# Narrower tiles for the third token tile, and a query projection that does not wait for the norm

## The reference

```python
h = rms(x, norm_mix)                     # x * rstd(x) * norm_mix, rstd is one number per token
proj = h @ w_in                          # split into lru, q_lat, kv_lat, k_rope, ret and mlstm parts
# B: latent attention
q = rms(q_lat, mla_q_norm) @ mla_wq_b    # q_lat is 256 wide
sc = (q_nope . k_nope + q_rope . k_rope) * scale ; p = softmax(sc + chunk mask) ; y_b = p @ v
# C: retention        att = (q k^T) * decay ;  y_c = att @ v + (q S) * cross ; S update
# D: mLSTM            ig, fg = m_if[:, 0:4] + b_i, m_if[:, 4:8] + b_f   (4 heads)
#                     sc = (q k^T) * exp(gates) ; y_d = sc @ v + g * (q C) ; C, n update
x += concat(head_rms(y_a..y_d) * gates) @ w_out
x += SwiGLU(rms(x, norm_ffn)) @ w_down
```

## Time and profile before

| | |
|---|---|
| median of 3 runs | 933.67 us (933.37 to 934.33) |
| the profiled execution | 933.06 us |
| its span, first to last instruction | 931.3 us |
| TensorE busy | 922.5 us, 99% |
| weight loads (PEld) | 811.5 us, 87% |
| VectorE, ScalarE, GpSimd busy | 495.3, 204.2, 444.4 us |
| granted TensorE clock, mean | 0.999 |

### The profile page before, as it was taken

One profiled execution on the slowest core, in us unless ns is written; L12 is line 12 of the kernel. 1 busy time (PEld: TensorE's weight loads), 2 busy tenths in 40 slices (PEclk: granted clock), 3 DMA queues, 4 the chain that ended last, 5 costly groups with the idle time before them and its releaser, 6 DMA issues.

```text
span 931.3 us, 14894 instructions
## 1 busy us (share of the span) xinstructions
PE 922.5 (99%) x5718; PEld 811.5 (87%) x5718; DVE 495.3 (53%) x1009; ACT 204.2 (22%) x445; POOL 444.4 (48%) x469
## 2 busy tenths in 40 slices
PE   8999999999999999999999999999999999999998
PEld 6777877777999999999977678777799999999998
DVE  5474656854565656512253565578357565563221
ACT  2224264531100000100031243562310000110001
POOL 6210380124966666676411205503168666666670
PEclk9999999999999999999999999999999999999999
DMA  9959412119544544443443773112555555534321
GB/s 279 231 132 69 141 47 91 50 15 253 137 136 137 137 137 139 133 146 125 123 128 108 61 147 95 46 48 50 124 149 140 142 144 144 148 123 135 126 95 41
DMA packets 159635, 113.02 MB, mean 121 GB/s; under 512 B 10246, under 2 KB 157356, under 8 KB 159436
## 3 DMA queue, kind: packets, MB, share of 16 engines
q1 hardware_dynamic: 154660, 104.50, 38.8%
q0 software_dynamic: 4272, 6.80, 7.1%
q10 hardware_dynamic: 632, 0.75, 0.3%
HBM read 108.46 MB, written 2.27 MB: 119 GB/s over the span
## 4 chain that ended last, share of the span: by engine, by line
PE 97%; DVE 1%; DMA 1%; ACT 0%; issue 0%; SPq 0%; ACTq 0%; DVEq 0%
PE ps L1128 52%; PE ps L776 20%; PE ps L1085 7%; PE ps L1146 2%; PE ps L885 1%; PE ps L857 1%; PE ps L982 1%; PE ps L922 1%; PE ps L1023 1%; PE ps L1032 1%; PE ps L804 1%; PE ps L824 1%; PE ps L965 1%; DMA arena<-in_x_sample 1%; PE ps L1043 1%; PE ps L1064 0%
## 5 line engine op out<-in xcount | busy, mean ns | idle before, releaser
L776 PE MATMUL ps<-hT,ring 128*128 128x320 f32 x672 | 187.8, 435 | 2.2 <-DVE hT L1597 1.7
L776 PEld LDWEIGHTS ps<-hT,ring 128*128 128x128 f32 x672 | 124.5, 190 | 54.8 <-DVE hT L1597 3.9
L601 POOL TENSOR_TENSOR work<-ring 128x512 f32<-128x512 f32 (+1 forms) x66 | 81.8, 1239 | 154.5 <-issue 113.3
L1128 PE MATMUL ps<-mixT,ring 128*128 128x160 f32 x672 | 105.0, 299 | 0.0
L1128 PE MATMUL ps<-hT,work 128*128 128x160 f32 x672 | 98.5, 299 | 0.0
L1128 PE MATMUL ps<-hT,ring 128*128 128x160 f32 x672 | 98.1, 299 | 0.0
L1128 PEld LDWEIGHTS ps<-mixT,ring 128*128 128x128 f32 x672 | 95.8, 190 | 0.0
L1128 PEld LDWEIGHTS ps<-hT,ring 128*128 128x128 f32 x672 | 93.7, 190 | 0.3
L1128 PEld LDWEIGHTS ps<-hT,work 128*128 128x128 f32 x672 | 93.7, 190 | 0.0
L603 POOL TENSOR_TENSOR work<-ring 128x512 f32<-128x512 f32 (+1 forms) x66 | 82.2, 1246 | 5.2
L602 POOL TENSOR_TENSOR ring<-ring 128x512 f32<-128x512 f32 (+1 forms) x66 | 82.2, 1246 | 5.2
(11 more groups left out here) (392 smaller groups left out, 1351.6 us busy)
## 6 DMA issues: line engine op xcount, KB each, us to landing
ring<-in_w_gu SPq DMA_DIRECT2D x88, 512.0 KB, 5.2
ring<-in_w_in SPq DMA_DIRECT2D x44, 512.0 KB, 7.1
ring<-in_w_down SPq DMA_DIRECT2D x32, 512.0 KB, 4.5
ring<-in_w_out SPq DMA_DIRECT2D x16, 512.0 KB, 4.5
ring<-in_w_down SPq DMA_DIRECT2D x16, 384.0 KB, 3.5
cst<-in_consts POOLq DMA_DIRECT2D x1, 1664.0 KB, 12.3
ring<-in_w_in SPq DMA_DIRECT2D x2, 640.0 KB, 5.5
arena<-r POOLq DMA_DIRECT2D x8, 160.0 KB, 17.0
```

Source lines behind the costliest of these rows:

```text
L601: step(tt(s3, a11, a21, ALU.subtract))
L776: ins = mm(bank(use, 0, T, m), w[:, k, c:c + m], hT[:, k, 0:T], start=(k == 0), stop=(k == KT - 1))
L1128: ins = mm(bank(use, at * HT, HT), left, right(k), start=(opens and k == 0 and at == 0), stop=(closes and k == n - 1), skip_group_check=True)
```

## The change

Four edits, in both layers.

1. Third token tile 64 wide. The third product of `causal_scores` takes 64 key columns as weights in place of 128; VectorE's part of it works on 64 partitions. L817 and L818 of `head_out` take 64 columns of weights and give 64 rows.
2. The turned probabilities. The five pieces that belong to the 64 stream tokens are turned from 64 partitions, 64 columns moving, and packed 64 wide; ScalarE copies 64 and 256 columns in place of 128 and 512.
3. The query latents are projected from `xgm = x * norm_mix` (in the memory of `mixT`), without `rstd`. VectorE multiplies by `rstd` afterwards, in two operations for each half (`qlat_raw`, then `qlT`), and ScalarE squares the first one's result. `xgm` is made by VectorE in layer 0 (8 operations ahead of `normalise`), by ScalarE in layer 1 (one after each square). In layer 1 half of `ql0` is moved ahead of the norm sum. The turn of the gain rows is moved in between the matmuls of `ms1`, and in layer 0 two of the `latents_out` stand ahead of the wait for `cols`. `kvr` now waits for all 8 pieces of `hT`.
4. The input and the forget gate are turned together: three transposes with the forget gate at partition 32 (`mgt`) in place of twice three (`mig`, `mfg`). `mift` is 64 wide and cleared at the start. With one use fewer in the list the later uses swap banks 0 and 1.

```diff
-SCORE_PARTS = ((0, 384), (448, 64))
+SCORE_PARTS = ((0, 384, P), (448, 64, DEC))
-    d("ql0", "ql1", "kvr", "mo0", "mo1", "mig", "mfg", "mv0", "mv1")
+    d("ql0", "ql1", "kvr", "mo0", "mo1", "mgt", "mv0", "mv1")
+        xgm = mixT
-        mift = sb("mift", [P, NT, 2 * H])
+        mift = sb("mift", [P, NT, 64])
@@ TensorE, the sum of ms1
+                if n == 4:
+                    pe.wait_ge(sem("gain_rows"), 16)
+                    nc.tensor.transpose(ps[:, 0, 0:NGAIN], rows[0:NGAIN, :], ident[0:NGAIN, 0:NGAIN]).then_inc(
+                        sem("rows_turned"), 1)
@@ feature
-                    if wait_h:
-                        need(pe, "normed", l, KT, k + 1)
-                    ins = mm(bank(use, 0, T, m), w[:, k, c:c + m], hT[:, k, 0:T], start=(k == 0), stop=(k == KT - 1))
+                    if right is not hT:
+                        pe.wait_ge(sem("mix_gained"), l * KT + k + 1)
+                    ins = mm(bank(use, 0, T, m), w[:, k, c:c + m], right[:, k, 0:T], start=(k == 0), stop=(k == KT - 1))
@@ causal_scores
-                fill(mm(bank(use, 448, 64), k[:, 256:384], q[:, 256:320], start=True, stop=True), use)
+                fill(mm(bank(use, 448, DEC, DEC), k[:, 256:256 + DEC], q[:, 256:320], start=True, stop=True), use)
@@ head_out
-                mm(o(2), w[:, 448:576], vaug[:, 2, h, 0:e], start=True, stop=False)
-                mm(o(2), cross, state, start=False, stop=True)
+                last = bank(use, 2 * e, e, DEC)
+                mm(last, w[:, 448:512], vaug[:, 2, h, 0:e], start=True, stop=False)
+                mm(last, cross, state, start=False, stop=True)
@@ order of TensorE at the start of a layer
                     latents_out(PAST_TILES[0:2])
+                    feature("ql0", l, "ql", 0, P, xgm, range(0, 4))
                     norm_sum("ms1", l)
+                    feature("ql0", l, "ql", 0, P, xgm, range(4, KT))
                     latents_out(PAST_TILES[2:])
...
+                    need(pe, "past_T", l, 1)
+                    latents_out(PAST_TILES[0:2])
                     pe.wait_ge(sem("cols_ready"), 2)
-                    need(pe, "past_T", l, 1)
-                    latents_out(PAST_TILES)
+                    latents_out(PAST_TILES[2:])
+                need(pe, "normed", l, KT)
                 claim(pe, "kvr", l)
@@ gates
-                for u, a in (("mig", 0), ("mfg", H)):
-                    claim(pe, u, l)
-                    need(pe, "mif_copied", l, 1)
-                    for t in range(NT):
-                        ins = nc.tensor.transpose(bank(u, t * P, P, H), mift[:, t, a:a + H], ident)
-                    fill(ins, u)
+                claim(pe, "mgt", l)
+                need(pe, "mif_copied", l, 1)
+                for t in range(NT):
+                    ins = nc.tensor.transpose(bank("mgt", t * P, P, 32 + H), mift[:, t, 0:32 + H], ident)
+                fill(ins, "mgt")
@@ turn_probs
-                    for a, w_, rr in ((0, 128, 128), (128, 128, 128), (256, 128, 128), (448, 64, 64),
-                                      (512, 128, 128), (640, 128, 128), (768, 128, 128), (896, 128, 128)):
-                        dst = bank(u, 384 if a == 448 else a, 128, rr)
-                        ins = nc.tensor.transpose(dst, pr[:, a:a + w_], ident)
+                    for a in range(0, 3 * P, P):
+                        nc.tensor.transpose(bank(u, a, P), pr[:, a:a + P], ident)
+                    nc.tensor.transpose(bank(u, 3 * P, DEC, DEC), pr[0:DEC, 448:512], ident[0:DEC, 0:DEC])
+                    for i in range(4):
+                        ins = nc.tensor.transpose(bank(u, 512 + i * DEC, DEC), pr[0:DEC, 512 + i * P:512 + (i + 1) * P],
+                                                  ident[0:DEC, 0:DEC])
@@ ScalarE
+                    if which == 0 and l > 0:
+                        A(xgm[:, k, :], xT[:, k, :], ACT.Copy, scale=col("norm_mix", l * KT + k)).then_inc(sem("mix_gained"), 1)
+                        act.wait_ge(sem("mix_gained"), l * KT + k + 1)
                 def latent_squares(p):
-                    wait_filled(act, f"ql{p}", l)
-                    step(A(qls[:, p, 0:T], bank(f"ql{p}", 0, T), ACT.Square), "qlat_sq")
+                    need(act, "qlat_raw", l, 2, p + 1)
+                    step(A(qls[:, p, 0:T], qls[:, p, 0:T], ACT.Square), "qlat_sq")
@@ VectorE
+                    for k in range(KT):
+                        v.tensor_scalar(xgm[:, k, :], xT[:, k, :], col("norm_mix", k), None, ALU.mult).then_inc(
+                            sem("mix_gained"), 1)
+                        dve.wait_ge(sem("mix_gained"), k + 1)
                 def query_latents(p):
-                    need(dve, "qlat_sq", l, 2, p + 1)
-                    step(v.tensor_scalar(qlT[:, p, 0:T], bank(f"ql{p}", 0, T), col("q_norm", 2 * l + p), None, ALU.mult))
+                    wait_filled(dve, f"ql{p}", l)
+                    step(v.tensor_tensor(qls[:, p, 0:T], bank(f"ql{p}", 0, T), rstd[:, :], ALU.mult), "qlat_raw")
+                    step(v.scalar_tensor_tensor(out=qlT[:, p, 0:T], in0=bank(f"ql{p}", 0, T), scalar=col("q_norm", 2 * l + p),
+                                                in1=rstd[:, :], op0=ALU.mult, op1=ALU.mult))
                     now_read(dve, f"ql{p}")
```

More of the change, by code:

```diff
@@ L454, in build, with row @@
         r = ROWS
-        def row(name, n, src):
-            SMALL.append((rows[r[name]:r[name] + n, 0:src.shape[-1]], src))
+        def row(name, n, src, at=0):
+            SMALL.append((rows[r[name]:r[name] + n, at:at + src.shape[-1]], src))
         row("norm_mix", DEPTH * KT, I["norm_mix"].rearrange("l (k p) -> (l k) p", p=P))
@@ L472, in build @@
         row("b_i", DEPTH, I["mlstm_b_if"][:, 0:H])
-        row("b_f", DEPTH, I["mlstm_b_if"][:, H:2 * H])
+        row("b_f", DEPTH, I["mlstm_b_if"][:, H:2 * H], at=32)
         GAINS, ROWLOADS, SMALL, CIN = SMALL[0], SMALL[1:], [], []
@@ L765, in norm_sum, with feature @@
                 fill(ins, use)
-            def feature(use, l, name, c, m, wait_h=False, ks=range(KT)):
+            def feature(use, l, name, c, m, right=hT, ks=range(KT)):
                 if ks[0] == 0:
@@ L999, in _ @@
                         need(pe, "qg_d", l, 1)
-                    head_out(f"do{h}", l, h, "w_d", HD + 1, ct[:, l, h, :], qg[:, h, :], True)
+                    head_out(f"do{h}", l, h, "w_d", HD + 1, ct[:, l, h, :], qg[:, h, 0:DEC], True)
                 def between(h):
@@ L1096, in _ @@
                         project(h - 2, (6, 7, 2, 3))
-                    head_out(f"co{h}", l, h, "w_c", HD, s0c[:, l, h // 2, :], qg[:, h, :], False)
+                    head_out(f"co{h}", l, h, "w_c", HD, s0c[:, l, h // 2, :], qg[:, h, 0:DEC], False)
                     if h == 0:
@@ L1399, in _ @@
                 step(A(small[:, 32:44], small[:, 56:68], ACT.Ln, scale=1.0 / ROPE, bias=eps_c[:, :]))
-                step(A(small[:, 20:44], small[:, 20:44], ACT.Exp, scale=-0.5), "q_rstd")
+                step(A(small[:, 20:44], small[:, 20:44], ACT.Exp, scale=-0.5), "q_stats")
                 for p in range(2):
@@ L1585, in _ @@
             step(v.memset(hT[:, :, T:TP], 0.0), "x_cleared")
-            for t in (kf[:, :, T:TP], wt[:, :, T:576], qg[:, :, DEC:P], r1[:, T:TP], nm[:, T:TP],
+            for t in (mift[:, :, :], kf[:, :, T:TP], wt[:, :, T:576], qg[:, :, DEC:P], r1[:, T:TP], nm[:, T:TP],
                       qh[:, :, :]):
@@ L1707, in _ @@
                     key_copies(PAST_TILES, 0)
+                latent_sum()
                 wait_filled(dve, "kvr", l)
                 kvr = bank("kvr", 0, 504).rearrange("p (t n) -> p t n", t=NT)
-                step(v.tensor_copy(mift[:, :, :], kvr[:, :, 160:168]), "mif_copied")
+                step(v.tensor_copy(mift[:, :, :].rearrange("p t (g n) -> p t g n", g=2)[:, :, :, 0:H],
+                                   kvr[:, :, 160:168].rearrange("p t (g n) -> p t g n", g=2)), "mif_copied")
                 step(v.tensor_copy(ckvn[:, :, :], kvr[:, :, 0:KVR]))
@@ L1870, in _ @@
                     wait_filled(dve, f"ds{h}", l)
-                    for a, n in SCORE_PARTS:
-                        step(v.tensor_tensor(wt[:, h % 2, a:a + n], bank(f"ds{h}", a, n), dh[:, h % 2, a:a + n], ALU.mult))
+                    for a, n, r in SCORE_PARTS:
+                        step(v.tensor_tensor(wt[0:r, h % 2, a:a + n], bank(f"ds{h}", a, n, r), dh[0:r, h % 2, a:a + n],
+                                             ALU.mult))
                     now_read(dve, f"ds{h}")
@@ L1985, in weights_c @@
                     wait_filled(dve, f"cs{h}", l)
-                    for a, n in SCORE_PARTS:
-                        step(v.tensor_tensor(wt[:, h % 2, a:a + n], bank(f"cs{h}", a, n), dec[:, h, a:a + n], ALU.mult),
+                    for a, n, r in SCORE_PARTS:
+                        step(v.tensor_tensor(wt[0:r, h % 2, a:a + n], bank(f"cs{h}", a, n, r), dec[0:r, h, a:a + n], ALU.mult),
                              "w_c" if a else None)
```

55 lines of the change are left out of this document (26 added, 29 removed).

## The result

| | before | changed |
|---|---|---|
| median | 933.46 us (933.04 to 935.17, 16 runs) | 935.92 us (934.52 to 936.79, 16 runs) |
| ratio | | 1.0024, 95% interval 1.0017 to 1.0030 |
| the profiled execution, its span | 933.06, 931.3 us | 935.48, 933.7 us |

The change costs 2.5 us. The forecast was 935.0, and the measured median lies 0.9 above it, inside the range. As a difference it does less well: +1.3 was forecast, and the measured one is nearly twice that. Of the three classes it is "slower by over 0.2%" by a hair (0.24%, with an interval that reaches from 0.17% to 0.30%), to which I had given 0.31 against 0.56 for "within".

The account below looks back on a forecast made before the run. TensorE was taken as the bound, 97% of the chain that ended last. Terms +1.9, +0.1, -1.3, +0.1 and +0.5 gave +1.3 us: 934.4 for the profiled execution, 935.0 for the median, range 932.2 to 937.3.

Parts of the forecast that it names:

- Part 1, third products: causal_scores and head_out: switching to 64-column weights and back outweighs the cheaper passes; +1.9 us, bounds -4.0 to +3.5.
- the first rival, narrow means cheaper: Third products and turned probabilities: a 64-wide pass costs 0.06 without any switch; sum -6.6 us, 927.1; chance 0.08.
- Part 2, turned probabilities: B heads: eight turns go from 0.87 to 0.85, or 0.91 with the uncovered load; taken as +0.1 us over 8 heads.
- The rival with dearer switches at the five small turns: Mainly B's turned probabilities: switches cost more than read, +2.4 in place of +0.1; sum +3.6 us, 937.3; chance 0.15.
- Part 4, gates: Gate turns in both layers: mv0 needs only the clamp of mo1 and starts 0.63 earlier, twice; -1.3 us.
- Part 3, start of layer 0: ql0 runs 1.6 us earlier, but TensorE then waits 2.3 for ScalarE's past_copy, queued behind a late square; +0.1 us.
- near 25.5: Sign in layer 0: after the wait for past_copy, the cache latents' products start near 25.5 us in the trace.
- if the cache arrives too late for L842: Start of layer 0: a cache load missing its turn at 21.6 makes it worse than the bounds -0.3 to +0.5.
- Part 3, start of layer 1: VectorE frees ql0's bank late, so kvr waits 1.5 us despite TensorE arriving 1.0 earlier; +0.5 us.
- the starts hold their gain: Rival: past_copy and ql0's bank in time, -1.6 and -1.0 in place of +0.1 and +0.5; sum -1.9, 931.8; chance 0.07.

Follow-up runs that it names:

- e1: The changed kernel with the third product of causal_scores back at 128 columns of weights: median 933.01 us, 931.7 at full clock.
- e2: The changed kernel with head_out's two third-tile products back at 128 columns in the D heads only: median 934.17 us, 934.1 at full clock.
- e4: The changed kernel with every narrow operand one column or partition wider, 65 in place of 64: median 926.70 us, ratio 0.9931 to the kernel before.
- e3: The changed kernel with the probabilities turned and copied in eight pieces of 128 again: median 936.30 us, 935.2 at full clock (two executions).
- e7: The kernel before with only the input and forget gates turned together and banks 0 and 1 swapped behind: median 932.00 us, ratio 0.9987.
- e6: The changed kernel with VectorE's two query-latent operations ahead of the first two key copies in layer 1: median 933.50 us, 933.3 at full clock.
- e11: The changed kernel run again unaltered, in the same rounds as e10: median 935.33 us, 934.6 at full clock.
- e10: The changed kernel with eight unused 128-column products filling TensorE's wait in layer 0, behind the turn of the parameter rows: median 934.59 us, ratio 1.0008.
- e5: The changed kernel with ScalarE's past_copy moved ahead of the squares of ql0 in layer 0: median 932.25 us, 932.2 at full clock.
- e9: e4 with the order changes of e5 and e6, and B's last stream products at 65 columns of weights: median 921.57 us, ratio 0.9875 to the kernel before.

## Why the prediction was right, and where it wasn't

Its own sum was +1.3 us. The two groups of executions compare with it like this: at full clock the changed kernel stands at 934.9, 1.4 over the 933.46 of the kernel before (1.6 over the 933.3 that it takes at full clock); and the second group moves the median of all by another 1.0. The first part was foreseen, nearly term by term; the second was not. The forecast of 935.0 was made from a median of three runs, 933.67, which lies 0.2 over that of sixteen: a small piece of luck, as from 933.46 the same sum gives 934.8.

**Part 1, third products (+1.9).** Right. `causal_scores` was worked out as 0.56 in place of 0.39, and measured as 0.57; `head_out` in D as +0.08 a head, measured +0.08; in C as -0.20, measured -0.22 (1.26 from L816 to L833, now 1.04 from L822 to L840). L811 takes 0.32, where 0.31 was asked for, and the start after L812 comes 0.25 later, as written. e1 and e2 give the same on the clock of the whole kernel: 3.2 (2.4 + 0.5 predicted) and 0.8. e4 takes the switches off by one column and keeps the cheaper passes. So the first rival, narrow means cheaper, fell on the switch alone: a pass costs 0.06, as it said, but a lone pair of passes did not earn its 0.22 of switching, nor did the two pairs of `head_out` in D. That the cost begins between 65 and 64 columns is shown; that it is a drain of the array is what fits it. The Trainium skill (TensorEngine Tiling (Array Packing), Key Properties) says that a change of tiling mode drains the array; the traces agree, with 0.22 for L811 in e1 and e4, where 128 or 65 columns of weights follow, and 0.32 in the changed kernel, where 64 do.

**Part 2, turned probabilities (+0.1).** Near: the turns take 0.84, where 0.85 was worked out, but the product behind them grew by 0.09 (0.23 to 0.32), where 0.06 was allowed. Together that is 1.16 against 1.10, +0.06 a head or +0.5 in all: 0.4 over the term and over its inner range of -0.2 to +0.3, inside the bounds of -1.9 to +2.4. The time of e3 can neither confirm nor deny 0.5. The rival with dearer switches at the five small turns (+2.4) is excluded by these rows.

**Part 4, gates (-1.3).** Right: -0.75 and -0.56 in the trace, -1.3 in e7.

**Part 3, start of layer 0 (+0.1).** The mechanism was right in each link: from L877 to L858 it was to take 2.4, and took 2.41. So the 1.6 us won ahead of `ql0` came back as a wait of 2.15 for `past_copy`, where 2.3 was written. The place in the trace, "near 25.5", held in five other profiles with this order (25.43 to 25.77, in e1, e2, e3, e4 and e6), but not in e11 (26.02), in e10 (26.77) and in the changed kernel's own: there L849 waited 0.78 for a load, and L877 stood 0.9 later. It comes close to the case named in the bounds ("if the cache arrives too late for L842"), though the bound of +0.5 was too tight for it, and what came too late was not the cache but the weights that are counted on the same semaphore. It accounts for some 0.9 of the profiled execution's 2.4, with the sum's 1.3. How much of the median it makes isn't shown: in the five executions at full clock that lie 0.3 to 1.1 over the quickest three, only the profiled one can be seen.

**What was missing: what an idle TensorE can do to its clock.** The prediction booked a wait at its length. Moving 1.7 us of idle time from one place to another and making it 2.15 was counted as an even trade. 13 of the changed kernel's 27 executions had the lower mean clock. In the profiled one of them TensorE came out of the wait at the lower level, and the products behind it took 1.7 more; that the other twelve lost it in the same place is likely, not seen. This is a term that no step of the sum had, worth about +1.0 on the first median. Without it the median would be 934.6 to 934.9, within 0.2% and in the class that I had thought likeliest.

**Part 3, start of layer 1 (+0.5).** Right: +0.45, with a wait of 1.29 ahead of `kvr` (1.5 written). The row gives no engine for what ended it ("issue"); VectorE's second operation ends at 486.30, 0.16 ahead of `kvr`, and e6 takes the wait away by the order of VectorE alone. With Part 1 at +1.9, Part 2 at +0.5, Part 4 at -1.3 and the start of layer 0 at 0 to +0.4, the terms as measured add to +1.5 to +1.9, where full-clock executions differ by 1.4 to 1.6.

The rival "the starts hold their gain" fell: it had both producers in time, and both were late for just the reason given against it. e5 and e6 show that it would have come true with two operations in another order.

## What to carry to other kernels

Narrowing an operand to 64 columns or partitions in the midst of full-width products cost 0.22 us here for each visit, on the way in and on the way out; read the product ahead of it and the one behind, and try 65, which kept the whole gain of the narrow passes and paid none of the switches. When an operation gets a new input, look at what is queued behind it on its own engine: in layer 0 a copy whose input was ready stood behind the late operation, in layer 1 the operation that frees the bank stood behind key copies, and both gains of the early starts were lost to that. And price idle time on TensorE by what comes after it as well as by its length.

## What the runs showed of the hardware

- Weights of 65 columns cost 0.11 to 0.12 for two passes of 64 or 65 moving columns, beside products 128 wide, with no switch (e4); two passes with weights of 64 columns between such products cost 0.25, and 0.10 on the product ahead. Of turns, five from 64 partitions made the group 0.84 and the next product 0.32; five from 65 partitions 0.63 and 0.28.
- A width of 65 columns doesn't help where the weights stand on 64 partitions: two such passes took 0.26 (e9).
- After 2.15 us without work TensorE's granted clock was 0.50 in three profiles (e3, e6, e11) and 1.00 in four others; the changed kernel had a mean clock of 0.998 in 13 of 27 executions. Eight passes of 512 columns took 5.40 us at the lower level, where they take 3.70 at full clock. With the same stretch filled by products that nobody reads, eleven of eleven had a mean of 0.999 or 1.0.
- e9's profiled execution had its drop elsewhere, at 8 to 10 us, behind 1.93 us without work while x was being turned; so there is more than one such place in this kernel.
